# Another order inside the steps of a mixer loop: level products before value products, outputs before the turn

## The reference, cut to what matters

```
def hybrid_mixer(h, w_in, ...):
    parts = jnp.split(h @ w_in, IN_SPLITS, axis=-1)
    ...
    o_nsa = nsa_group(...)      # per head: softmax(q k) v over keys, windowed keys, compressed keys
    o_hg = hgrn2_group(...)     # per head: decayed q k products (a) times values, then norm and gate
    return jnp.concatenate([o_nsa, o_hg], axis=-1) @ w_out
```

## Time and profile before

| what | value |
|---|---|
| median of 3 runs | 1681.82 us (1681.73 to 1685.08) |
| the profiled execution's own time | 1682.07 us |
| its span | 1680.8 us |
| PE busy, share of the span | 98% |
| DVE busy | 71% |
| ACT busy | 52% |
| mixer loop on PE | about 290 us to 355 us of the span |

### The profile page before, as it was taken

The page is one execution under the profiler, slowest core; times in us unless marked ns, Lnnn a source line. Parts: engine busy times, 40 slices in busy tenths (PEclk is TensorE's granted clock), DMA queues, the critical chain, the costliest instruction groups (busy, mean ns, idle before and its releaser), DMA issues.

```text
span 1680.8 us, 24145 instructions
## 1 busy us (share of the span) xinstructions
PE 1639.8 (98%) x9640; PEld 1424.6 (85%) x9640; DVE 1189.7 (71%) x1991; ACT 878.0 (52%) x1521; POOL 50.8 (3%) x87
## 2 busy tenths in 40 slices
PE   7999999999999999999999999999999999999997
PEld 6888899778888888889888888888888998888886
DVE  5666757956666676676877676786667787676777
ACT  4544456755444454445755444554444666454445
POOL 0000000101000000001210000000000000000000
PEclk9999999999999999999999999999999999999999
DMA  9555346034555455545445555555554433555541
GB/s 367 188 188 188 140 176 251 1 121 172 192 192 193 166 205 190 190 157 221 157 176 197 189 190 179 221 181 198 188 188 182 151 145 126 198 219 189 189 163 50
DMA packets 32111, 301.54 MB, mean 179 GB/s; under 512 B 3824, under 2 KB 4352, under 8 KB 6016
## 3 DMA queue, kind: packets, MB, share of 16 engines
q1 hardware_dynamic: 32000, 300.01, 48.6%
HBM read 298.93 MB, written 1.06 MB: 178 GB/s over the span
## 4 chain that ended last, share of the span: by engine, by line
PE 87%; DVE 7%; ACT 4%; issue 1%; POOL 0%; DMA 0%; SPq 0%; DVEq 0%; ACTq 0%
PE bank L477 28%; PE bank L467 27%; PE bank L466 12%; PE bank L456 9%; PE bank L469 2%; DVE w_lo L429 1%; PE bank L507 1%; PE bank L2073 1%; PE bank L579 1%; DVE x L847 1%; PE bank L580 1%; PE bank L604 1%; PE bank L2075 1%; PE bank L583 1%; PE bank L1670 1%
## 5 line engine op out<-in xcount | busy, mean ns | idle before, releaser
L429 DVE TENSOR_TENSOR w_lo<-w_raw,w_hi 128x1024 fp32r<-128x1024 f32 (+4 forms) x539 | 586.7, 1138 | 191.0 <-ACT w_hi L422 190.5
L467 PE MATMUL bank<-xT,w_hi 128*128 128x512 f32 x1920 | 673.9, 396 | 0.3 <-DVE w_lo L429 0.3
L422 ACT ACTIVATE w_hi<-w_raw 128x1024 fp32r<-128x1024 f32 (+5 forms) x543 | 500.2, 981 | 98.3 <-PE bank L477 82.2
L466 PE MATMUL bank<-xT,w_lo 128*128 128x256 f32 x1680 | 468.4, 279 | 0.0
L467 PEld LDWEIGHTS bank<-xT,w_hi 128*128 128x128 f32 x1920 | 351.6, 188 | 69.9 <-DVE w_lo L429 0.5
L466 PEld LDWEIGHTS bank<-xT,w_lo 128*128 128x128 f32 x1680 | 316.7, 189 | 10.4
L794 ACT ACTIVATE ff_silu<-ff_silu 128x256 f32<-128x256 f32 x124 | 51.9, 419 | 387.8 <-DVE ff_silu L934 387.8
L477 PE MATMUL bank<-w_hi,hT_hi 128*128 128x512 f32 x480 | 187.5, 391 | 0.0
L477 PE MATMUL bank<-w_lo,hT_hi 128*128 128x512 f32 x480 | 186.8, 389 | 0.0
L477 PE MATMUL bank<-w_hi,hT_lo 128*128 128x512 f32 x480 | 186.8, 389 | 0.0
L934 DVE TENSOR_REDUCE ff_silu<-bank 128x256 f32<-128x512 f32 x124 | 85.6, 691 | 101.7 <-PE bank L467 100.6
(11 more groups left out here) (398 smaller groups left out, 2167.3 us busy)
## 6 DMA issues: line engine op xcount, KB each, us to landing
w_raw<-in_ffn_a SPq DMA_DIRECT2D x22, 1536.0 KB, 6.4
w_raw<-in_ffn_b SPq DMA_DIRECT2D x22, 1536.0 KB, 6.5
w_raw<-in_ffn_c SPq DMA_DIRECT2D x22, 1536.0 KB, 6.4
w_raw<-in_ffn_d SPq DMA_DIRECT2D x22, 1536.0 KB, 6.4
w_raw<-in_ffn_e SPq DMA_DIRECT2D x22, 1536.0 KB, 6.5
w_raw<-in_ffn_f SPq DMA_DIRECT2D x22, 1536.0 KB, 6.4
gains<-in_gains SPq DMA_DIRECT2D x11, 1024.0 KB, 5.1
w_raw<-in_mla_up SPq DMA_DIRECT2D x8, 1280.0 KB, 5.6
```

The costliest lines, as they stand in the source:

```text
L422: nc.scalar.activation(hi, src, ACTF.Copy).then_inc(w_hi_made, 1)
L429: nc.vector.tensor_tensor(lo, src, hi.bitcast(F32), ALU.subtract).then_inc(w_lo_made, 1)
L466: nc.tensor.matmul(o[:, 0:SEQ], lo[:, c], xT[:, k, 0, :], start=False, stop=False)
L467: ins = nc.tensor.matmul(o, hi[:, c], xT[:, k, :, :], start=(k == 0), stop=(k == KD - 1))
```

## The change

In PE's loop `level_products(k)` comes before `values(k-2)`, and `outputs(k-1)` comes before `turn_output(k-2)`. On ACT `value_hi(k-2)` goes from before `weights(k)` to behind it, and `keep_output(k-1)` comes before `output_hi(k-2)`. On DVE `mask_levels(k)` comes before `value_lo(k-2)` and the decay work behind it. No instruction is added, removed or changed in size, and no semaphore or count changes.

```diff
@@ pe_mixer
             for k in range(STEPS):
                 scores(k)
+                level_products(k)
                 if k >= 2:
                     values(k - 2)
-                level_products(k)
+                if k >= 1:
+                    outputs(k - 1)
                 if k >= 2:
                     turn_output(k - 2)
                 if k >= 1:
-                    outputs(k - 1)
                     turn_weights(k - 1)
@@ act_mixer
-                if k >= 2:
-                    value_hi(k - 2)
                 if k == 1:
                     copy_cross(k)
                 if k < STEPS:
                     weights(k)
+                if k >= 2:
+                    value_hi(k - 2)
                 if 1 < k < STEPS and k % 2:
                     copy_cross(k)
+                if 1 <= k <= STEPS:
+                    keep_output(k - 1)
                 if k >= 2:
                     output_hi(k - 2)
                 if 1 <= k <= STEPS:
-                    keep_output(k - 1)
                     copy_weights(k - 1)
@@ dve_mixer
+                if k < STEPS:
+                    mask_levels(k)
                 if k >= 2:
                     value_lo(k - 2)
...
                     right(3)
                     left(3)
-                if k < STEPS:
-                    mask_levels(k)
```

## The result

The changed kernel takes 1691.78 us (median of 6 runs, 1691.2 to 1692.74) against 1681.78 us before (6 runs). The ratio is 1.0056 with a 95% interval of 1.0046 to 1.0066: slower by 0.46 to 0.66%. The forecast was 1689.1 us, in a range of 1685 to 1693. The profiled execution took 1691.77 us with a span of 1690.5 us, 9.7 us more than before.

What follows compares the result with a forecast made beforehand. PE was taken to bound the kernel (87% of the span), with DVE also full in steps 3 to 5. 1682.07 + 5.6 (order) + 1.7 (clock) = 1689.4 us, as a median 1689.1 us; range 1685 to 1693.

Steps and rivals of the forecast that it cites:

- What bounds: Whole kernel: PE bounds it; behind the loop no idle time takes up a delay, so loop changes reach the end.
- `value_hi` behind the exponentials: ACT, each loop step: `value_hi` starts at s + 4.63 us and `value_lo` on DVE at s + 5.1.
- The turn's wait: PE before `turn_output`: waits for `value_lo` until s + 5.65, some 0.85 us, making a three-engine loop of 8.7 us.
- DVE's wait: DVE before `value_lo`, until s + 5.1: steps 3 to 5 each grow by 1.15 us.
- The order's term: Loop: the waits from the new order make it end 5.6 us later, bounds 4.8 to 6.5.
- The term that was too small: PE's clock after the 5.4 us idle in step 2: a slow stretch costing 1.7 us, bounds 0 and 3.1.
- The upper bound of 3.1 us: Slow clock in step 2: turn, weights and scores(3), 3.1 us at full clock, all run at half rate.
- Further falls of the clock: Rival, loop steps 3 to 7: two or three more slow stretches, 1 to 4 us more, 1690 to 1693; chance 0.20.
- Not slower: Rival, PE's turn in the loop: it doesn't have to wait, 1.6 us less, 1680.2 us; chance 0.16.

Runs made afterwards that it cites:

- e2: The changed kernel with the gated output turned into its own bank 4, so the turn no longer waits for `value_lo`; ratio 1.0021 to the kernel before.
- e7: As e2, and on DVE the decay work of steps 2 to 5 goes ahead of `value_lo`; ratio 1.0013 to the kernel before.
- e1: The changed kernel with 20 idle products on PE in the wait before `turn_output(0)`; ratio 1.0032 to the kernel before.
- e8: As e7, with `left(2)` and `left(3)` moved to GpSimd and 9 idle products on PE in step 2's wait; ratio 1.0007 to the kernel before.
- e10: The kernel before with 10 idle products ahead of `values(0)` and 13 of 18 instructions of DVE's `away(2)` moved to GpSimd; ratio 1.0000 to it.
- e5_act_dve_only: The changed kernel with PE's old order, so only ACT's and DVE's orders are new; ratio 1.0078 to the kernel before.

## Why the prediction was right

**The mechanism, by its steps.** *What bounds*: the loop's 9.6 us came through to the end (span +9.7). *`value_hi` behind the exponentials*: shown, s + 5.02 in step 4 against s + 5.1. *The turn's wait* and *DVE's wait*: both seen where they were said to be; e2 took away the first and e7 the second on top of it. *The order's term*: 5.6 us forecast, 5.61 measured (e1 against before). That isn't luck, since every piece of the sum fits: in e1 the steps from s(2) are 8.66, 9.42, 9.16, 10.23 and 8.66 us, and 6.68 from s(7) to the end; forecast were 8.7, 9.4, 9.1, 10.3, 8.7 and 6.65.

**The term that was too small.** "A slow stretch as short as the 3.40 us one costs half its length, 1.7; I take that." Measured by e1_warm: 4.0 us. The stretch lasted 10.2 us. For the choice of the short row the sum gave no reason: the nearer row, the stretch of 6.80 us in the same step of the kernel before, halves to 3.4. The upper bound of 3.1 us was wrong as well, because it counted only turn, weights and scores(3). These made step 2 longer by 2.71 us, inside the bound. Then step 3 was long too, 10.69 us instead of 9.42: the level products were still at half clock (319.19 to 322.5), so `values(1)` began only at 323.19, and ACT, done with its exponentials, waited for it in front of `value_hi`:

```profile
319.19 2.07 PE L1164 MATMUL bank<-mix_logs 128*128 128x128 f32 x8
...
323.19 0.65 PE L1150 MATMUL bank<-lent_x,mix_vals 128*64 128x256 f32 x2
```

```profile
325.31 0.38 ACT L1338 ACTIVATE mix_oT_hi<-bank 64x256 fp32r<-64x256 f32 x1 [1.29 <-PE bank L1152]
```

A delay that had been hidden behind ACT came out once PE was slow enough. The Trainium skill's rule on the clock ("TensorE: Matmul & The Clock Gate", "HAM oscillation — how this bites in real kernels") prices a throttled stretch at half its length, 5.1 us here, as an estimate. The trace agrees with the half rate. PE idled 1.2 us of that stretch, which leaves half of 8.99, 4.5 us; the 4.0 measured are less, and where the other 0.5 was hidden no run shows. That the whole came out below the upper end of the range, 1693, is in part luck: it had been set for further falls of the clock, and none came.

**A term that was missing.** PE's own work in the new order is 8.14 us a step, 0.19 more, with the same instructions. It is hidden wherever PE waits anyhow, so it doesn't show in the change's total; it shows in e7 and e8. By the timeline of e8, step 4, level products take 1.98 us instead of 1.89 and outputs 1.22 instead of 1.11, now that values follow the ones and precede the others; what makes it was not tested.

**The rivals.** Further falls of the clock in steps 3 to 7: none (0.99 from 322.50 on), although PE idled 0.5 to 1.5 us a step from step 4. Not slower: out, the turn waits in every step but step 3, where PE was the late one.

## What to carry to other kernels

A move in one engine's list is priced on the other engines' lists: find who waits for the moved piece, and what stands in the list in front of the thing it now stands behind. Here a 0.4 us copy behind 2.35 us of exponentials opened a loop through three engines. A wait that is hidden by another moves, it does not vanish: step 2 exchanged 2.64 us for 0.49 and 5.04 us. And when a change makes the matrix engine idle longer once, count a slow clock for all that runs until it is back, with what is then late on the other engines, not for the first few products alone. Products that are there only to keep the clock up are no remedy once it has fallen: in e10 they ran at half rate and held up the work behind them.

## What the runs showed of the hardware beyond that

The length of a slow stretch doesn't follow from the length of the wait. With the wait of 5.04 us the clock was at half for 10.2 us, while PE was busy 8.99 us of them; with 2.64 us of idle time it had been 6.8 us. With the same wait of 2.70 us it was 10.1 us in e2_own_bank and 7.1 us in e7_own_bank_lo_late, PE busy throughout both (the two rows under e7). Waits of 0.5 to 1.5 us a step left it at full in the changed kernel, and so did the five of 1.26 to 1.63 us in e5_act_dve_only, where the one of 2.17 us did not; but in e8 it fell around a wait of 0.85 us, some 4 us behind one of 0.90 us.

GpSimd beside VectorE slows it: eight elementwise products of 128x128 took 1.71 us with GpSimd idle (`left(2)` before, 319.47 to 321.1), 2.13 us with GpSimd busy for a part, 3.42 us with it busy throughout. The Trainium skill says that GpSimd's SBUF interfaces are shared with VectorE, with contention for VectorE instructions with two SBUF inputs ("GPSIMD Engine Reference", "1. Specifications"); these are such, and the runs agree.
